# A step of a hybrid decoder on one core: where four groups of VectorE work and the matmuls that read it stand in the order of the dense part

## The reference

```python
h = rms_norm(x, norm1_g) * (1 + sc1) + sh1
z = h @ w_in                                  # a_val, a_gt, b_u, b_v, c_b, c_c, c_h, gates
a = a_val * sigmoid(a_gt); a, _ = causal_dwconv(a, hist_a, a_dw_w)     # 31 taps
a = silu(layer_norm(a + a_dw_b, a_norm_g, a_norm_b, CONV_A_GROUPS))
u = gelu(b_u); v = layer_norm(gelu(b_v), b_norm_g, b_norm_b)
bb = u * chunk_spatial_mix(v, b_spatial_w, b_spatial_b)
ch, _ = causal_dwconv(c_c * c_h, hist_c, c_conv_w); cc = c_b * ch
br = einsum('ntgc,gcd->ntgd', stack([a, bb, cc], axis=2), w_branch)
mixed = sum(sigmoid(gates) * br, axis=2) @ w_out
x = x + g1 * mixed
h2 = rms_norm(x, norm2_g) * (1 + sc2) + sh2   # then router, top-1 group, top-2 of its 8 experts
x = x + g2 * hier_moe(h2); y = rms_norm(x, final_norm_g)
```

## Time and profile before

| what | value |
|---|---|
| median of 3 runs | 1747.78 us (1747.28 to 1748.83) |
| the profiled execution, its own time | 1748.83 us |
| its span, first to last instruction | 1747.1 us |
| TensorE matmuls busy | 1586.5 us, 91% |
| VectorE busy | 1266.9 us, 73% |
| ScalarE busy | 804.4 us, 46% |
| mean granted TensorE clock | 0.949 of full speed |

### The profile page before, as it was taken

One profiled execution on the slowest core, in us unless ns is written; L12 is line 12 of the kernel. 1 busy time (PEld: TensorE's weight loads), 2 busy tenths in 40 slices (PEclk: granted clock), 3 DMA queues, 4 the chain that ended last, 5 costly groups with the idle time before them and its releaser, 6 DMA issues.

```text
span 1747.1 us, 23198 instructions
## 1 busy us (share of the span) xinstructions
PE 1586.5 (91%) x9110; PEld 1363.1 (78%) x9110; DVE 1266.9 (73%) x1703; ACT 804.4 (46%) x867; POOL 237.2 (14%) x235
## 2 busy tenths in 40 slices
PE   4999999999998999999899974999999999999940
PEld 2666677688788999998799974888888888888830
DVE  3667777745846598877444345989899998989848
ACT  3212232234333123222142333788888787878823
POOL 1310000000000000002000211254412222121200
PEclk8899999999999999999899985999999999999985
DMA  9846222424323322234122535899999999999854
GB/s 328 269 151 200 75 74 86 137 61 153 109 88 129 110 85 79 67 90 128 49 79 86 200 122 223 308 391 394 392 378 375 378 374 387 373 385 397 319 232 175
DMA packets 215759, 368.48 MB, mean 211 GB/s; under 512 B 15110, under 2 KB 163654, under 8 KB 190298
## 3 DMA queue, kind: packets, MB, share of 16 engines
q1 hardware_dynamic: 197724, 327.95, 52.8%
q0 software_dynamic: 17856, 38.99, 6.2%
q10 hardware_dynamic: 70, 0.05, 0.0%
HBM read 353.45 MB, written 31.20 MB: 220 GB/s over the span
## 4 chain that ended last, share of the span: by engine, by line
PE 82%; DVE 11%; DVEq 3%; issue 2%; ACT 2%; DMA 1%; POOL 0%; POOLq 0%; SPq 0%; ACTq 0%
PE z L2357 14%; PE z L2359 14%; PE z L2358 14%; PE z L713 7%; PE z L715 7%; PE z L714 7%; PE z L730 3%; PE z L731 3%; PE z L732 3%; DVE conv L1860 2%; PE q L704 2%; DVE yin L935 1%; PE q L2255 1%; PE q L2274 1%; PE q L721 1%
## 5 line engine op out<-in xcount | busy, mean ns | idle before, releaser
L935 DVE TENSOR_TENSOR wl<-wr,whr 128x2048 fp32r<-128x2048 f32 x198 | 444.2, 2285 | 0.0
L2357 PE MATMUL z<-h_hi,w_hi 128*128 128x272 f32 (+1 forms) x1248 | 411.8, 330 | 0.0
L2359 PE MATMUL z<-h_hi,w_lo 128*128 128x272 f32 (+1 forms) x1248 | 406.9, 326 | 0.0
L2358 PE MATMUL z<-h_lo,w_hi 128*128 128x272 f32 (+1 forms) x1248 | 406.5, 326 | 0.0
L852 ACT ACTIVATE whr<-wr 128x2048 fp32r<-128x2048 f32 x198 | 376.2, 1913 | 37.7 <-PE z L715 32.2
L1691 DVE TENSOR_TENSOR w_lo<-w_raw,w_hi 128x1024 fp32r<-128x1024 f32 (+1 forms) x168 | 179.4, 1069 | 161.8 <-ACT w_hi L1430 161.8
L2357 PEld LDWEIGHTS z<-h_hi,w_hi 128*128 128x128 f32 x1248 | 237.6, 190 | 31.6 <-issue 13.7
L2359 PEld LDWEIGHTS z<-h_hi,w_lo 128*128 128x128 f32 x1248 | 236.9, 190 | 18.4
L2358 PEld LDWEIGHTS z<-h_lo,w_hi 128*128 128x128 f32 x1248 | 237.3, 190 | 17.6 <-issue 0.2
L713 PE MATMUL z<-whr,xTh 128*128 128x512 f32 x528 | 209.7, 397 | 2.4 <-DVE xTl L935 2.4
L715 PE MATMUL z<-wl,xTh 128*128 128x512 f32 x528 | 206.8, 392 | 0.0
(11 more groups left out here) (373 smaller groups left out, 2192.3 us busy)
## 6 DMA issues: line engine op xcount, KB each, us to landing
wr<-in_w_dram SPq DMA_DIRECT2D x198, 1024.0 KB, 7.8
w_raw<-in_w_in_dram SPq DMA_DIRECT2D x104, 512.0 KB, 3.7
ada<-in_w_ada_dram SPq DMA_DIRECT2D x6, 2048.0 KB, 12.1
w_raw<-in_w_branch_dram SPq DMA_DIRECT2D x48, 256.0 KB, 2.7
w_raw<-in_w_out_dram SPq DMA_DIRECT2D x16, 512.0 KB, 3.9
yin<-y_rows SPq DMA_DIRECT2D x16, 512.0 KB, 9.6
ada_h<-in_w_ada_dram SPq DMA_DIRECT2D x2, 2048.0 KB, 15.5
ada_u<-in_w_ada_dram SPq DMA_DIRECT2D x2, 2048.0 KB, 10.1
```

The lines of the kernel that those rows point to most:

```text
L935: return dve.tensor_tensor(out, a, b, op)
L2357: pe.matmul(out, w_hi[w][:, k, :], hi[:, k, t0:t1], start=(k == 0), stop=False)
L2358: pe.matmul(out, w_hi[w][:, k, :], lo[:, k, t0:t1], start=False, stop=False)
L2359: last = pe.matmul(out, w_lo[w][:, k, :], hi[:, k, t0:t1], start=False, stop=(k == kn - 1))
```

## The change

1. The rows of h2 of group 0 use one buffer `h2s[0]` instead of four; `tail_h2` waits from the second tile on until the store of the tile before has landed and PE has transposed it.
2. In group 1, `h2_transpose(i)` moves from behind item A0+2i+1 to ahead of it, and `logits(i)` from behind item A0+2i+2 to behind item A0+2i+1. ACT's `tail_tile(i)` moves ahead of one weight rounding, DVE's `tail_logits(i)` from the next pair to the same one. ACT's wait for the tail moves ahead of the C0 chunks.
3. `v_stats` moves behind `gated` of pair 0 of GC0, `v_norm` of tiles 0 and 1 behind pair 1, of 2 and 3 behind pair 2, of the sample tile behind pair 3. PE's `spatial` waits for all of them at once, and starts behind pair 3 instead of behind pair 2. DVE's `spatial(t)` moves from ahead of `gated` of pair 3+t to behind `gated` of pair 4+t.
4. `states` moves from behind item GB0 to ahead of it.
5. `normed(0)` and `normed(1)` move from ahead of `gated` of GB0 pair 5 to behind it, `normed(2)` and `normed(3)` likewise at pair 6.

```diff
-                pool.dma_start(h2_dram[r0:r0 + rows, :], h2s[t][0:rows, :]
+                pool.dma_start(h2_dram[bass.ds(r0, rows), :], h2s[s][0:rows, :]
...
             def tail_h2(g, t, rows=P, factors=None):
-                if g and t == 0:
+                if g == 0 and t:
+                    dve.wait_ge(h2_out, t * 16)
+                    q_wait_ready(dve, "h2T", 0, t - 1)
+                elif g and t == 0:
...
-                        if i:
-                            tail_logits(0, i - 1)
+                        tail_logits(0, i)
...
                 q_wait_read(dve, "vT", g, CW - 1)
-                v_stats()
-                v_norm((0, 1))
                 for i in range(KD):
-                    if PT - 1 <= i < 2 * PT - 1:
-                        spatial(i - PT + 1)
-                    elif g and i == KD - 1:
-                        spatial(PT, SMP)
                     gated(NB_C, GC0, i)
                     if i == 0:
-                        v_norm((2, 3))
-                    elif g and i == 1:
-                        v_norm((PT,))
+                        v_stats()
+                    elif i < 3:
+                        v_norm((2 * i - 2, 2 * i - 1))
+                    elif i == 3:
+                        if g:
+                            v_norm((PT,))
+                    else:
+                        spatial(i - PT)
                     conv_step(g, 2, (2, 3))
+                if g:
+                    spatial(PT, SMP)
...
                 def silus(cs):
+                    normed(cs[0])
                     for c in cs:
+                        if c + 1 in cs:
+                            normed(c + 1)
...
                 gated(NB_B, GB0, 4)
-                normed(0)
-                normed(1)
                 gated(NB_B, GB0, 5)
                 silus([0, 1])
-                normed(2)
-                normed(3)
                 gated(NB_B, GB0, 6)
...
                         if i == 0:
                             out_transpose(0, KD // 2 - 1, 0)
                             out_transpose(0, KD // 2 - 1, 1)
-                        else:
-                            logits(i - 1)
+                        h2_transpose(i)
                     item(g, A0 + 2 * i + 1, h_hi, h_lo)
                     if g:
-                        h2_transpose(i)
+                        logits(i)
...
-                pairs(GC0, 0, PT - 1, act0_hi, act0_lo)
+                pairs(GC0, 0, PT, act0_hi, act0_lo)
...
-                    pe.wait_ge(vn_ok, PT * g + t + 1)
+                    pe.wait_ge(vn_ok, PT + g * (PT + 1))
...
-                for i in range(PT - 1, KD):
-                    if i - PT + 2 < PT:
-                        spatial(i - PT + 2)
-                    elif g and i == 2 * PT - 2:
+                for i in range(PT, KD):
+                    if i - PT + 1 < PT:
+                        spatial(i - PT + 1)
+                    elif g:
                         spatial(PT, SMP)
```

More of the change, by code:

```diff
@@ L1344, in _, with tail_out @@
                     bias_load(i + 2)
-            def tail_out(g, t, rows):
+            def tail_out(g, t, rows, s=0):
                 r0 = t * P + g * PT * P
                 pool.dma_start(x1_dram[bass.ds(r0, rows), :], chunk(xres, t)[0:rows, :]).then_inc(x1_out, 16)
-                pool.wait_ge(h2_ok, PT * g + t + 1)
-                pool.dma_start(h2_dram[r0:r0 + rows, :], h2s[t][0:rows, :]
+                n_ = before_wait(pool, PT * g + t + 1)
+                pool.wait_ge(h2_ok, n_)
+                pool.dma_start(h2_dram[bass.ds(r0, rows), :], h2s[s][0:rows, :]
                                ).then_inc(h2_last[t % 2] if g else h2_out, 16)
@@ L1392, in _ @@
             for t, rows in tiles(1):
-                tail_out(1, t, rows)
+                tail_out(1, t, rows, t)
             moe_gpsimd(pool)
@@ L1522, in a_chunk @@
                     ahead(g, A0 + 2 * i)
-                    if g == 0 and i == 0:
+                    if g:
+                        tail_tile(i)
+                    elif i == 0:
                         par_read()
-                    elif g == 0 and i == 1:
+                    elif i == 1:
                         hist_read()
                     ahead(g, A0 + 2 * i + 1)
-                    if g:
-                        tail_tile(i)
                 if g:
@@ L1548, in c_chunk @@
                             act.wait_ge(z_free[s], slot_use(g, uk) + 1)
-                            if g and i == 0:
-                                act.wait_ge(h2_out, 16 * PT)
-                                q_wait_read(act, "lg", 0, PT - 1)
                             act.activation(chunk(act0_hi, i)[:, 0:T], cv[:, 0:T], ACT.Copy).then_inc(chi_ok, 1)
+                if g:
+                    act.wait_ge(x1_sq, PT)
+                    act.wait_ge(h2_out, 16 * PT)
+                    q_wait_read(act, "lg", 0, PT - 1)
                 for i in range(CW):
@@ L1877, in tail_h2 @@
                 scale, shift = factors or (A2, B2)
-                if g and t == 0:
+                if g == 0 and t:
+                    dve.wait_ge(h2_out, t * 16)
+                    q_wait_ready(dve, "h2T", 0, t - 1)
+                elif g and t == 0:
                     dve.wait_ge(h2_out, PT * 16)
                     q_wait_ready(dve, "h2T", 0, PT - 1)
-                h = h2s[t][0:rows, :]
+                h = h2s[t if g else 0][0:rows, :]
                 dve.scalar_tensor_tensor(h, xres[0:rows, t, :], r2y[0:rows, t:t + 1], scale[0:rows, :], ALU.mult, ALU.mult)
@@ L1981, in c_chunk @@
                     last.then_inc(z_free[sc], 1)
-                    if g and i == 0:
-                        tail_logits(0, PT - 1)
                     ahead(g, i0 + 1)
@@ L2365, in h2_transpose @@
                 for k in range(KD):
-                    last = transposed(q[s][:, k // 4, (k % 4) * P:(k % 4 + 1) * P], h2s[t][:, k * P:(k + 1) * P])
+                    last = transposed(q[s][:, k // 4, (k % 4) * P:(k % 4 + 1) * P], h2s[0][:, k * P:(k + 1) * P])
                 last.then_inc(q_ready[s], 1)
@@ L2453, in _ @@
                     item(g, C0 + i, h_hi, h_lo)
-                    if g and i == 0:
-                        logits(PT - 1)
                     if g == 0:
@@ L2506, in _ @@
                 spatial(0)
-                for i in range(PT - 1, KD):
-                    if i - PT + 2 < PT:
-                        spatial(i - PT + 2)
-                    elif g and i == 2 * PT - 2:
+                for i in range(PT, KD):
+                    if i - PT + 1 < PT:
+                        spatial(i - PT + 1)
+                    elif g:
                         spatial(PT, SMP)
                     pairs(GC0, i, i + 1, act0_hi, act0_lo)
-                def states():
+                if g:
                     for name, src, n in (("stA", a_tail, HA), ("stC", p_tail, HC)):
@@ L2550, in _ @@
                 item(g, GB0, h_hi, h_lo)
-                if g:
-                    states()
                 pe.wait_ge(blo_ok, CW * (g + 1))
```

## The result

The changed kernel takes 1813.6 us (median of 4 runs, 1811.3 to 1816.5), against 1747.9 us before in the same comparison: ratio 1.0373, 95% interval 1.0357 to 1.0391. It is slower by 65.7 us. The profiled execution took 1812.1 us with a span of 1810.4, which is 63.3 us more than the span before; the mean granted clock fell from 0.949 to 0.937. VectorE was busy for 1267.0 us against 1266.9: no work was added, it was only moved.

What follows compares the result with a forecast made beforehand. TensorE, holding 82% of the chain that ended last, was taken as the bound. Waits of 42.9 us, with the clock 56.6, on the profiled 1748.83 gave 1805.4; the median 1 us lower, so 1804, range 1792 to 1815.

Steps and rivals of the forecast that it cites:

- second rival: TensorE: every wait drops the clock, and transposes behind the long ones hold it down longer: 1811 us, chance 0.15.
- the sum: Whole kernel: added waits of 42.9 us, with the clock 56.6 us, giving 1804 us; chance 0.50 as it stands.
- GB0 branch, group 0: Input of GB0's branch in group 0: TensorE waits 2.2 us in place of 0.5, cost 1.7 us.
- z waits that go: First `gated` of GC0: early release of z[1] gives back waits of 1.6 us (group 0) and 2.3 us (group 1).
- Steps 1 and 2: h2 tail, start of group 1: first wait grows by 6.1 us, three later tiles cost 3.9; sum 10.0 us.
- Step 3: Later layer norm of v and `spatial` in GC0: 5.9 us in group 0, 11.5 us in group 1.
- Step 4: Conv states ahead of item GB0: TensorE waits for q[0], held by the sample tile of `spatial`; cost 6.0 us.
- Step 5: Conv branch norm in GB0: third `spread` late by 3.7 and 3.5 us, z[0] by 1.0 and 1.3; sum 9.5 us.
- The taps' waits do not shrink: GB0 of group 1: waits of 4.2 and 4.9 us stay, since VectorE's taps start behind item GB0+1.
- third rival: GB0 taps: if VectorE entered with its taps ahead, the 9.1 us of waits would vanish: 1795 us, chance 0.10.
- The clock: Half clock on TensorE: 2.9 us behind each of two long waits, 1.7 for two in three of seven shorter; 13.7 us.
- first rival: TensorE: short waits keep the clock, none of the seven of 2.9 to 3.7 us drops it: 1796 us, chance 0.18.

Runs made afterwards that it cites:

- e1: Kernel before with only the single h2 buffer and the tail's transposes and logits earlier on TensorE: 1751.3 us, ratio 1.0037.
- e10: Same kernel as e1 plus ten matmuls that nobody reads ahead of TensorE's wait for the last h2 rows: 1750.3 us, ratio 1.0013.
- e9: Kernel before with ten matmuls that nobody reads ahead of TensorE's wait for the last h2 rows of group 1: 1748.2 us, ratio 0.9998.
- e5: Changed kernel with four h2 buffers again, its order kept: 1814.2 us, ratio to the kernel before 1.0369.
- e2: Kernel before with only the layer norm of v and the position mixing (`spatial`) moved later: 1778.4 us, ratio 1.0170.
- e3: Kernel before with only the conv `states` moved ahead of item GB0: 1749.5 us, ratio 1.0004.
- e12: Kernel before with the later layer norm of v and position mixing, and `states` ahead of item GB0: 1787.6 us, ratio 1.0225.
- e4: Kernel before with only `normed` moved behind `gated` in GB0: 1761.2 us, ratio 1.0071.
- e6: Changed kernel with matmuls that nobody reads set into its new holes on TensorE: 1792.7 us, ratio to the kernel before 1.0251.
- e8: Same kernel as e7 plus more VectorE taps in pairs 4 to 7 of GC0: 1737.7 us, ratio to the kernel before 0.9941.
- e7: Kernel before with only `v_stats` and all `v_norm` moved behind `gated` of pairs 0 to 2, TensorE's order kept: 1754.7 us, ratio 1.0033.
- e11: Same kernel as e8 plus ten unread matmuls ahead of the last h2 wait and twenty in the 5.2 us hole: 1728.9 us, ratio 0.9883.

## Why the prediction was right, and where a size was off

The forecast was 1804 us in a range of 1792 to 1815; 1813.6 lies near its upper end, which came from the second rival and not from the sum. Sign and mechanism held, and the waits held nearly one by one:

| step | forecast of waits, us | measured |
|---|---|---|
| first h2 tile, the three others | 11.3; 3 x 1.3 | 11.3; 4.0 together |
| `spatial` from the third tile on | 5 x 2.9 | 5.5 (two), 8.4 (three) |
| `spatial(0)` of group 1 | 6.8 | 6.9 |
| GB0 branch, group 0 | 2.2 | 2.0 |
| `a_tail` transposes | 6.0 | 6.1 |
| third `spread` | 3.5 and 3.7 | 3.4 and 4.0 |
| sigmoid of pair 7 | 1.3 and 1.0 | 2.5 for both, 1.4 the first |
| z waits that go | 1.6 and 2.3 | gone |

- *Steps 1 and 2*: 10.0 us forecast; e1 shows 10.4 in the dense part and e10 against e9 10.6. That the buffer costs nothing is shown by e5. Not foreseen was that an execution can win 8 to 10 us back in the last logits; the changed kernel's profile shows no such gain (h2 rows to router 27.65 us in both).
- *Step 3*: 17.4 us forecast, which is 19.1 us of waits less 1.7 of clock; the waits are as listed. e2 shows them alone: 20.5 us more idle time, with the 1.9 us wait that was not foreseen.
- *Step 4*: the wait is right, and e3 with e12 show its condition: none alone, 6.1 us behind step 3.
- *Step 5*: 9.5 us forecast, 9.5 measured in e4. For the third `spread` of group 1 the prediction says 3.7 us; its own rows (882.05 + 0.72 less 879.2) give 3.6, which e4 has too.
- *The taps' waits do not shrink*: in group 1 right (4.2 and 5.2 against 4.2 and 4.9). In group 0 the waits at `mean` shrank from 3.8 to 2.6 us, a little of the third rival.
- *The clock* is the term that was too small. Of the forecast's 13.7 us, 1.7 had already been taken off in the sum of step 3, so that 12.0 more were forecast. Measured are 18.1 more, or 21.3 without the stage that nothing touches; e6 gives back 20.9 us when the holes are filled. The step that failed is "1.7 us for two in three of the seven waits of 2.9 to 3.7 us". A half-clock stretch stood behind each of the seven. They cost 1.7, 1.6 and 1.5 us in group 0 and 3.1, 1.7, 3.2 and 4.2 us in group 1, together 17.0 in place of 7.9: besides coming every time, three of them lasted 6.8 or 10.2 us and not 3.4. One stood behind the 2.0 us wait too, and cost 1.7. The second rival (every wait drops the clock, 1811 us, given 0.15) was the better account, though in other profiles not every such wait does: of the twenty waits of 2.8 us at `spatial` in those of the changed kernel, e2, e5 and e12, eighteen were followed by half clock within 1.5 us and two were not. The first rival, and with it the Trainium skill's advice (TensorE: Matmul & The Clock Gate, "Why this matters for your kernels") against gaps of more than about 3 us, taken as if shorter ones cost nothing, is refuted here: all five waits of 2.8 us in the changed kernel's profile were followed by half clock.
- The rest. Waits alone were forecast at 42.9 + 1.7 = 44.6 us and measured at 45.2. The 9.1 us by which the rise of 65.7 exceeds the forecast's 56.6 are 0.6 of waits, 6.1 of clock, and 2.4 between the median's rise (65.7) and the span's (63.3), which is the spread of executions; the 0.6 us that the windows do not place and the 0.6 us by which the expert part is shorter cancel.

The parts alone add up to 3.1 + 30.3 + 1.3 + 13.0 = 47.7 us, the whole is 65.7. Two shares of the missing 18.0 are seen: the 6.1 us wait that step 4 has only behind step 3 (3 to 9 us in all), and the 7 to 9 us that e1 wins back in the last logits, which the changed kernel does not. How they divide the 18.0, and whether anything else is in it, is open.

## What to carry to other kernels

If a small piece of work on one engine stands right behind the item that its releaser also waits for, its wait is the releaser's whole path from that item, however idle the releaser is: put reads of a finished result ahead of the instruction that waits for the next item. The cost of a move can depend on another move, so reckon them together. On TensorE do not charge a wait by its length alone: read from the trace whether half clock follows, and for how long. Behind nearly all waits of 2.8 us here it did, and added 1.6 to 3.2 us to each in the changed kernel. And look for idle time on the engine whose work is waited for later, as e8 did with 0.6% from moved taps.

## What the hardware showed beyond what was expected

- Around 2 us the length of a wait did not tell whether half clock follows; the same wait went either way. The 1.93 us wait at `mean` of group 0 was followed by it in the changed kernel, e1, e3, e4, e5 and e9, and not in the kernel before, e6, e7 and e10. The 2.3 us wait of the earlier trace rows was followed by it in the kernel before, e1, e3 and e10, and not in e4 and e9.
- The clock also fell with no wait ahead. In the kernel before, the matmuls of two columns in `variance` of group 1 ran from 850.8 to 856.2 us with TensorE busy throughout, 16 us behind the last wait; the clock fell at 853.4 and stayed at half for 6.8 us, which cost 3.4. The prediction has no such term. The windows (length, busy, instructions, granted clock, DMA):

```profile
852.00:853.00 1.00, 1.00 (x11) 1.00 0.79 237
853.00:854.00 1.00, 1.00 (x9) 0.74 0.95 282
```

- About 100 transposes and logits of 36 columns ran for 20 us at half clock without bringing it back, in the kernel before, the changed one and e9; where the clock was up when they began, or rose right after, the same work took some 9 to 10 us less (e1, e10, e11). The executions of e1 fall in two groups, 1747 to 1753 and 1760 to 1764 us, as if it went either way there too.
- The clock before GC0 of group 0, in a part that no version changes, cost between 2.7 and 9.1 us in the executions profiled. Differences of a few microseconds between profiles need this in mind.
